# A hybrid decoder step on one core: the closing steps of an HGRN head get a buffer of their own and a later place on VectorE

## The reference, cut to what matters

```python
def gla_chunk(state, inp):
    q, k, v, g = inp
    bcum = jnp.cumsum(g, axis=2)
    inter = jnp.einsum('bhtk,bhkv->bhtv', q * jnp.exp(bcum), state)
    diff = jnp.where(causal, bcum[:, :, :, None, :] - bcum[:, :, None, :, :], -jnp.inf)
    att = jnp.einsum('bhtk,bhtsk,bhsk->bhts', q, jnp.exp(diff), k)
    o = inter + jnp.einsum('bhts,bhsv->bhtv', att, v)
    ...

def hgrn_out(o, gate, g_norm, w_out):
    o = rmsnorm(o.transpose(0, 2, 1, 3), g_norm).reshape(b, s, B_WIDTH).astype(gate.dtype)
    return (o * jax.nn.silu(gate)) @ w_out
```

## Time and profile before

| | us |
|---|---|
| median of 3 runs | 2405.84 |
| the profiled execution | 2406.53 |
| its span, first to last instruction | 2404.7 |
| PE busy in the span | 2279.9 |
| DVE busy | 1245.0 |
| ACT busy | 1099.6 |
| POOL busy | 726.5 |

### The profile page before, as it was taken

How to read it: one execution, slowest core, us unless ns; L and a number is a source line. 1 busy time by engine, 2 the same in 40 slices (tenths; PEclk the granted TensorE clock), 3 DMA queues, 4 the chain that set the end, 5 groups by cost and what they waited for, 6 DMA issues and landing times. The chain is left out here.

```text
span 2404.7 us, 47436 instructions
## 1 busy us (share of the span) xinstructions
PE 2279.9 (95%) x17886; PEld 1889.8 (79%) x17886; DVE 1245.0 (52%) x1971; ACT 1099.6 (46%) x1874; POOL 726.5 (30%) x810
## 2 busy tenths in 40 slices
PE   7999999999989999999987989999999999999999
PEld 7956666666688999999976979989997676666658
DVE  4134556566443667766666155675212355655552
ACT  4155544554344444545553146664212654445541
POOL 1234322333030223322224314552321532322311
PEclk9999999999999999999987999999999999999999
DMA  4020433434332111111102211111113033434333
GB/s 162 18 76 4 127 111 107 116 100 117 114 113 72 46 55 39 54 55 47 54 21 78 74 45 40 42 46 53 62 36 134 13 92 111 119 97 116 110 106 141
DMA packets 104282, 187.69 MB, mean 78 GB/s; under 512 B 15722, under 2 KB 84332, under 8 KB 102916
## 3 DMA queue, kind: packets, MB, share of 16 engines
q1 hardware_dynamic: 104068, 184.81, 24.6%
HBM read 164.84 MB, written 19.92 MB: 77 GB/s over the span
## 5 line engine op out<-in xcount | busy, mean ns | idle before, releaser
L1617 POOL TENSOR_TENSOR latents_t_lo<-pages_t,latents_t_hi 128x256 fp32r<-128x256 f32 x256 | 187.7, 733 | 551.7 <-ACT latents_t_hi L1858 551.0
L2020 DVE TENSOR_REDUCE sums<-w_uq 128x8 f32<-128x512 f32 x256 | 175.2, 684 | 264.5 <-ACT w_uq L1866 264.2
L1866 ACT ACTIVATE w_uq<-ps 128x512 f32<-128x512 f32 x256 | 152.8, 597 | 211.3 <-PE ps L1702 210.5
L2323 PE MATMUL ps<-src_hi,w_hi 128*128 128x344 f32 x720 | 240.4, 334 | 3.0 <-ACT normed L2479 2.6
L1702 PE MATMUL ps<-w_uk_hi,latents_t_hi 128*128 128x512 f32 x512 | 236.6, 462 | 1.2 <-POOL latents_t_lo L1617 1.2
L2323 PE MATMUL ps<-src_hi,w_lo 128*128 128x344 f32 x720 | 231.6, 322 | 0.0
L2323 PE MATMUL ps<-src_lo,w_hi 128*128 128x344 f32 x720 | 231.4, 321 | 0.0
L1702 PE MATMUL ps<-w_uk_lo,latents_t_hi 128*128 128x512 f32 x512 | 204.0, 398 | 0.0
L1702 PE MATMUL ps<-w_uk_hi,latents_t_lo 128*128 128x512 f32 x512 | 203.6, 398 | 0.0
L1875 ACT ACTIVATE latents<-ps,bias,rq 128x256 f32<-128x256 f32 (+7 forms) x128 | 106.1, 829 | 131.2 <-DVE bias L2034 117.5
L831 PE MATMUL ps<-carried_src,w_hi 128*128 128x344 f32 x816 | 153.4, 324 | 11.5 <-DVE carried_src L887 9.2
(11 more groups left out here) (375 smaller groups left out, 5382.5 us busy)
## 6 DMA issues: line engine op xcount, KB each, us to landing
pages_t<-in_pages_t SPq DMA_DIRECT2D x256, 208.0 KB, 2.6
pages<-in_pages SPq DMA_DIRECT2D x256, 128.0 KB, 2.1
w_slots<-in_w_hgrn SPq DMA_DIRECT2D x30, 512.0 KB, 3.6
w_slots<-in_w_mla_in SPq DMA_DIRECT2D x17, 512.0 KB, 3.6
x_home<-residual SPq DMA_DIRECT2D x2, 4128.0 KB, 14.8
w_slots<-in_w_rg SPq DMA_DIRECT2D x14, 512.0 KB, 3.4
residual<-in_x SPq DMA_DIRECT2D x8, 516.0 KB, 8.6
residual<-in_x SPq DMA_DIRECT2D x1, 4128.0 KB, 13.6
```

Source lines behind the costliest of these rows:

```text
L1617: nc.gpsimd.tensor_tensor(lat_lo[:, g % DEPTH, :, :].rearrange("p k t -> p (k t)"), ring[:, g % RING, 0:KVL], lat_hi[:, g % DEPTH, :, :].r ...
L1866: nc.scalar.activation(sq[:, g % 2, :], keys(g), ACT.Square).then_inc(squared, 1)
L2020: nc.vector.tensor_reduce(ss[:, b % 2, p, :], sq[:, g % 2, :].rearrange("p (h d) -> p h d", h=H), AX.X, ALU.add).then_inc(ssum, 1)
L2323: mm = nc.tensor.matmul(bank[:, 0:TT], w[:, slot, kk, :], x[:, kk, cols], start=(kk == 0 and m == 0), stop=(kk == KD - 1 and m == 2))
```

## The change

The squares and the root get a buffer of their own (`root`, one row of 1032 numbers in each partition); it is allocated last in its stage, and no other buffer of the stage moves. POOL's wait for the finish ahead of level 1 goes, since `z[:, 1]` is no longer held. On DVE the call of `finish` moves from behind pick(0) and `weight_lo` to behind the third selection, pick(2), ahead of the next `weight_lo`. Instructions, their shapes and their number stay the same on every engine.

```diff
-        sqo = z[:, 1, :]
-        rs = z[:, 1, :]
+        rs = sqo = st.sb("root", [P, T])[:, :]
...
                     pool.wait_ge(exped, 17 * h + (2 * l + 2))
-                    if l == 1:
-                        wait(pool, og_done, h)
...
                     else:
                         weight_lo(H, 1)
-                    finish(h - 1, 1 - u)
                 dve.wait_ge(scanned, 8 * h + 2)
                 upper(1)
...
                         upper(l)
                         pick(l)
+                    if l == 2 and (not isinstance(h, int) or h > 0):
+                        finish(h - 1, 1 - u)
                     if following is not None and l in (2, 5):
```

## The result

The changed kernel takes 2432.35 us in the median of 4 runs (2430.49 to 2434.13), the kernel before 2406.45 beside it (2404.24 to 2410.53). The ratio is 1.0108, interval 1.0092 to 1.0125: slower by 25.9 us, where 19.2 were forecast. The direction and the place are as forecast; the time lies 0.35 us above the upper end of the range.

The account below looks back on a forecast made before the run. PE, busy 95% of the span, was taken to bound the kernel. 14.2 - 1.5 + 3.5 + 2.8 = 19.0 us on the profiled 2406.53 gave 2425.5, forecast as 2425 us; range 2411 to 2432.

Parts of the forecast that it names:

- level 3 waits for the finish: Heads 1 to 6, before level 3: the moved finish adds its own 2.36 us a head, 14.2 us in all.
- levels 1 and 2 no longer wait: Heads 1 to 6: PE's 7.2 us of waits there shrink to 0.95 us a head, a gain of 1.5 us.
- clock in heads 1 to 6: The longer idle stretch at level 3 drops PE's clock in three of six heads, two more than now: 2.8 us.
- last head: the finish: Head 7: the finish costs between its own 2.36 us and 4.8 with two more waits; 3.5 taken.
- elsewhere: Rest of the kernel: nothing else was expected to move on the path.
- the rival of half speed: DVE and POOL run side by side at half speed: 1.3 us a head instead of 2.36, 2417 us; chance 0.12.
- the rival that the finish hides beside the addition: Before level 3 the finish fits beside POOL's addition, so the kernel is not slower: 2403 us; chance 0.08.
- the 28 that were named as a sign: PE's idle time before the level products of heads 1 to 6 should rise from 15.4 to about 28 us.
- not to 70: Sign in the profile after: loop heads should take 70 us.
- one in each: Upper bound of the clock step: a fall in each of heads 1 to 6, five more than now, 7.0 us.
- the rival of six falls: The clock falls in each of heads 1 to 6: 24.5 us slower, 2430 us; chance 0.10.

Follow-up runs that it names:

- e4: The changed kernel, but POOL's addition of the sample states stands behind its lower half of level 4 instead of level 2: 2415.93 us, ratio 1.0044.
- e1: The changed kernel with the finish back in its old place behind pick(0); new buffer kept, POOL's wait still out: 2409.94 us, ratio 1.0012.
- e10: The changed kernel run a second time in a later session, nothing altered: 2434.32 us, ratio 1.0114.
- e5: The changed kernel, but in head 7, the last, the finish of head 6 stands in its old place behind pick(0): 2431.35 us, ratio 1.0086.
- e3: The changed kernel with 18 unused matmuls in each of heads 0 to 6, where PE waits for level 3: 2419.01 us, ratio 1.004.
- e2: The changed kernel, but the finish stands behind pick(5), the sixth selection, instead of behind pick(2): 2403.69 us, ratio 0.9984.

## Why the prediction was right and where it failed

The table sets the terms of the sum beside what the profiled execution shows; the measured terms add up to its 27.5 us but for rounding.

| term | forecast | measured |
|---|---|---|
| level 3 waits for the finish | +14.2 | +12.9 |
| levels 1 and 2 no longer wait | -1.5 | -4.2 |
| clock in heads 1 to 6 | +2.8 | +10.7 |
| last head: the finish | +3.5 | +3.9 |
| last head: the clock in its outputs | 0 | +1.1 |
| elsewhere | 0 | +3.0 |

**The moved finish: right.** The waits before level 3 add up to 8.2 us before and 21.05 after. In heads 1, 3 and 6 they are 3.71 to 3.76 us, 2.28 more than 1.43 to 1.49, where 2.36 was worked out. In heads 2, 4 and 5 they are 3.25 to 3.30: there the unit ahead ran at half clock and ended later, so that less waiting was left. The ends of the two engines, and e4's 1.28 us without the addition beside it, speak for turns, and the rival of half speed is out: with it the waits would have grown by 1.3 us. So is the rival that the finish hides beside the addition: its products took 3.4 to 3.5 and 2.0 to 2.2 us. Each product ends 1.09 us behind the POOL instruction beside it. This is the exclusive lock of the Trainium skill's page "SBUF — State Buffer", section "SBUF: two separate sides", which VectorE and GpSimd hold for a whole instruction each; the trace agrees, here and in e1.

**Levels 1 and 2: right where the clock did not fall behind the spread.** 0.95 us was left to each head, from head 0. In heads 1, 3 and 6 level 2 still waits 1.04, 1.04 and 0.94 us; in heads 2, 4 and 5 it does not wait at all. These are the heads whose clock fell behind the spread: PE, slower there, comes later itself. That is no gain, since the time is in the clock's term. It is also why the idle time came to 24.1 us and not to the 28 that were named as a sign. That the heads came to 71.2 to 72.1 us and not to 70 is the fall behind level 3 in each of them.

**The clock: the step that failed.** The step reads "I take three of six, two more than now: 2.8 us", with "one in each" as its upper bound, 7.0 us net. The count was wrong: all six heads fall behind level 3, in three executions out of three (the change, e10 and e5). The price of a fall came out right, 1.4 us taken from head 4 before against 1.55 from e3, but in part by luck: the fall of head 4 stood behind the spread and lasted 6.8 us, those behind level 3 mostly last 3.4.

Three heads fall a second time, behind the spread (one in e5), which no bound had foreseen. This adds nothing to their length: heads 4 and 5, with two falls, take 71.4 and 71.3 us, heads 1 and 6, with one, 71.2 and 71.3. PE then waits less before levels 2 and 3, 4.4 us less in heads 2, 4 and 5 together than in the other three. The 10.7 us of the table are what is left of the 19.4 once 8.7 of idle time is taken off, so they hold these second falls too. The miss that lengthened the heads is the count behind level 3: six falls at 1.55 less the 1.4 of before are some 7.9 us, by this estimate, where 2.8 stood.

The argument against the rival of six falls, that head 3 before kept a clock of 1.00 with waits of the same kind, did not carry: those waits were 0.3, 0.7 and 1.4 us at three levels, while now one of 3.7 us stands in a single place, followed by small products alone. That rival's 2430 us comes nearest to the result, and e3 shows its mechanism: fill the wait, and the six falls go.

**The last head: nearly right in size.** 3.9 us up to its outputs (3.5 against e5), where 3.5 was taken as the middle of a range of 2.36 to 4.8. On the way the finish did come to stand against a low part of POOL's, as one end of that range had it: the difference for level 4 takes 3.37 us behind it. What brought the whole head to 5.1 was a half-clock stretch of 6.8 instead of 3.4 us in its outputs.

**Elsewhere.** The 3.0 us are 1.3 in head 0, where the half-clock stretch lasts 6.8 us instead of 3.4, 0.8 less ahead of it, and 2.5 in the stages behind the heads, which the change does not touch. They take 1093.4 us before, 1096.0 after, but 1093.2 in e10 and 1090.5 in e1, so this looks like chance, and no forecast could have named it. With it left out the profile stands 24.5 us above before.

**Still open.** Why the clock falls behind the spread in one set of heads or another (one before, three in the change and in e10, one in e5, four in e1, where the finish stands in its old place), and what decides a fall at waits of 1.85 us (e4, where two heads of three fell).

## What to carry to other kernels

Before an instruction is moved on an engine off the critical path, list what stands behind it in the new place, and what POOL runs beside it there: the finish, 2.6 us in a free stretch (e2), held up both engines where POOL's addition stood (e4). A wait that PE gets in one piece can cost its length and then the clock behind it: before level 3, waits of 3.25 to 3.77 us did so in every head, those of up to 1.49 us in none. Where the trace shows half-clock stretches at all, count one for each repetition of a gap as long, and look for work to fill it. And a wait that looks like waste can order two engines' turns: taking POOL's out gained nothing, because its product then ran in the middle of the finish (e1).

## What the runs showed of the hardware that was not expected

- Freed from a wait, a POOL product of 1.3 us put 0.75 to 0.96 us onto the VectorE product that it came to stand beside (from 1.23 to between 1.98 and 2.19 us, e1).
- Added matmuls, 108 in heads 1 to 6 with 18.0 us of PE's time, made the kernel faster: ratio 1.004 against 1.0108, with the clock of these heads at 0.99 instead of 0.96 (e3).
- The same 39 matmuls of the last head took 5.8, 7.4 or 8.5 us at mean clocks of 1.00, 0.77 and 0.66, with 0.8 us of idle time in each.
